# Second modulation moved from TensorE to ScalarE and GpSimd, and other units outside the ring

## What is computed

```python
mod = (silu(c) @ w_ada + b_ada).reshape(b, 6, 1, d)
shift1, scale1, gate1, shift2, scale2, gate2 = ...
h = rms_norm(x, norm1_g) * (1 + scale1) + shift1
proj = h @ w_in                      # conv, stick-breaking and forgetting heads
...                                  # attention of 6 + 6 heads, short convolution
x = x + gate1 * (y @ w_out)
h2 = rms_norm(x, norm2_g) * (1 + scale2) + shift2
x = x + gate2 * moe_ffn(h2, ...)     # per expert: w_mlp1 1024x2048 (8 MB), w_mlp2 1024x1024 (4 MB)
```

## Time and profile before

| | us |
|---|---|
| median of 3 runs | 1621.92 |
| the profiled execution | 1622.58 |
| its span | 1620.8 |
| TensorE busy | 1522.6 (94%) |
| VectorE busy | 669.7 (41%) |
| ScalarE busy | 456.2 (28%) |
| GpSimd busy | 113.7 (7%) |

### The profile page before, as it was taken

How to read it: one execution, slowest core, us unless ns; L and a number is a source line. 1 busy time by engine, 2 the same in 40 slices (tenths; PEclk the granted TensorE clock), 3 DMA queues, 4 the chain that set the end, 5 groups by cost and what they waited for, 6 DMA issues and landing times.

```text
span 1620.8 us, 21577 instructions
## 1 busy us (share of the span) xinstructions
PE 1522.6 (94%) x8585; PEld 868.8 (54%) x8585; DVE 669.7 (41%) x969; ACT 456.2 (28%) x760; POOL 113.7 (7%) x125
## 2 busy tenths in 40 slices
PE   7999999999999998999998989887999999999998
PEld 4888533333333333333332323223858998899986
DVE  4676632323322232232222222224866665465654
ACT  3565311011101110111110110003765444454443
POOL 4132200000000000000000000000520002200000
PEclk9999999999999999999999999998999999999999
DMA  9977999999999999999999999999537555465520
GB/s 352 381 217 274 385 385 426 426 409 415 426 426 426 426 425 427 427 425 425 427 426 426 425 426 426 426 424 346 187 104 223 188 190 191 143 210 183 182 104 27
DMA packets 113394, 534.27 MB, mean 330 GB/s; under 512 B 7013, under 2 KB 70140, under 8 KB 87376
## 3 DMA queue, kind: packets, MB, share of 16 engines
q1 hardware_dynamic: 111232, 529.97, 82.6%
q0 software_dynamic: 2000, 1.98, 0.4%
HBM read 530.87 MB, written 1.05 MB: 328 GB/s over the span
## 4 chain that ended last, share of the span: by engine, by line
PE 43%; DMA 17%; DVE 4%; ACT 2%; issue 1%; DVEq 0%
DMA ring<-in_w_mlp 17%; PE ps L1021 8%; PE ps L576 8%; PE ps L578 8%; PE ps L577 8%; PE ps L1039 5%; PE ps L1046 1%; PE ps L1478 1%; PE ps L1469 1%; DVE ps L2364 1%; DVE wm L1638 1%; PE ps L992 1%; DVE arena L2139 0%; DVE arena L2132 0%; DVE arena L2135 0%
## 5 line engine op out<-in xcount | busy, mean ns | idle before, releaser
L1021 PE MATMUL ps<-ring,arena 128*64 128x512 f32 x2024 | 483.8, 603 | 20.2 <-DMA ring<-in_w_mlp 18.5
L1021 PEld LDWEIGHTS ps<-ring,arena 128*64 128x64 f32 x2024 | 129.1, 136 | 255.7 <-issue 210.4
L1039 PE MATMUL ps<-ring,arena 128*64 128x512 f32 x1024 | 231.0, 597 | 16.6 <-DMA ring<-in_w_mlp 10.3
L1638 DVE TENSOR_TENSOR wl<-ring,wh 128x1024 fp32r<-128x1024 f32 x132 | 161.9, 1232 | 136.1 <-ACT wh L2527 136.1
L576 PE MATMUL ps<-hth,wh 128*128 128x256 f32 x704 | 201.0, 285 | 0.9 <-DVE htl L2319 0.8
L577 PE MATMUL ps<-htl,wh 128*128 128x256 f32 x704 | 198.7, 282 | 0.0
L578 PE MATMUL ps<-hth,wl 128*128 128x256 f32 x704 | 198.1, 281 | 0.0
L2119 DVE TENSOR_TENSOR arena<-ps,arena 128x1024 f32<-128x1024 f32 x68 | 83.2, 1224 | 251.6 <-PE ps L1046 246.1
L2527 ACT ACTIVATE wh<-ring 128x1024 fp32r<-128x1024 f32 x132 | 139.3, 1060 | 148.9 <-PE ps L578 148.8
L1039 PEld LDWEIGHTS ps<-ring,arena 128*64 128x64 f32 x1024 | 75.2, 137 | 164.7 <-issue 140.4
L2144 DVE TENSOR_TENSOR arena<-ps,arena 128x512 f32<-128x512 f32 x34 | 23.5, 691 | 334.0 <-PE ps L1039 330.9
(11 more groups left out here) (457 smaller groups left out, 1851.4 us busy)
## 6 DMA issues: line engine op xcount, KB each, us to landing
ring<-in_w_mlp SPq DMA_DIRECT2D x187, 2048.0 KB, 27.5
ring<-in_ffn_w_gate SPq DMA_DIRECT2D x22, 1024.0 KB, 5.4
ring<-in_ffn_w_up SPq DMA_DIRECT2D x22, 1024.0 KB, 5.4
ring<-in_ffn_w_down SPq DMA_DIRECT2D x22, 1024.0 KB, 4.8
ring<-in_w_ada SPq DMA_DIRECT2D x16, 1024.0 KB, 9.5
ring<-in_w_ada SPq DMA_DIRECT2D x16, 512.0 KB, 11.2
ring<-in_w_mlp SPq DMA_DIRECT2D x8, 1024.0 KB, 33.1
ring<-in_w_in SPq DMA_DIRECT2D x10, 768.0 KB, 12.7
```

Source lines behind the costliest of these rows:

```text
L1021: t = pe.matmul(PS[64 * g:64 * g + 64, HB[hb][ns], :], x[:, k8, :], u[:, f:f + 512], start=False, stop=k8 == 7)
L1039: t = pe.matmul(PS[64 * g:64 * g + 64, 3, :], a4[:, kc, 64 * kg:64 * kg + 64], u[:, c, g * 512:(g + 1) * 512], start=k8 == 0, stop=k8 == 7)
L1638: dve.tensor_tensor(l, src, h.bitcast(F32), ALU.subtract).then_inc(*V.tick((st, "lo", n)))
```

## The change

Five things at once:

- The eight units of the second modulation no longer go through TensorE. ScalarE multiplies each with its 128 values of silu(c) (`ada_scaled`, 128x2048, in place in the ring; unit 0 into slot 15, `row_sums`), VectorE adds `b_ada` to partition 0 of the sum, and GpSimd adds units 1 to 7 to `row_sums` (`summed`). So the sum over the 128 partitions is still open.
- It is made where it is used: gate1 by a product with ones (`gate_row`), shift2 by eight products with a column of ones, in place of `mod_row` and the four transposes.
- Unit k's slot is free only when GpSimd has added it, and slot 15 when shift2 is turned. `front_order` places the eight units one at a time between later pieces.
- Expert 0's last two w1 units are loaded into the ring. Outside stand w2 (0,3), loaded after the router's parts, and w1 (1,3), after "HL upper"; w2 (0,2) and w1 (1,2) come alone. For expert 0 `AT` lies elsewhere, and VectorE waits for its second pass ahead of the output.
- One DMA brings the 2048 biases instead of four; `conv_w_2` is loaded after expert 0's w2.

```diff
 def front_order():
-    for n, mods in enumerate(((0,), (1,), (2, 3), (4, 5), (6, 7))):
-        order += [("ada", 1, k) for k in mods] + [("in", *units[n])]
-    return order + [("in", *u) for u in units[5:]]
+    for n, k in enumerate((None, 0, 1, 2, 3, None, 4, 5, 6, 7, None)):
+        order += ([] if k is None else [("ada", k)]) + [("in", *units[n])]
+    return order
...
         if n == experts:
-            slots, at = [14, 15, 12, 13, 0, 1, 2, 3, 4, 5, 6, 7, 8, 9, 10, 11], 0
+            slots, at = [12, 13, 0, 1, 2, 3, 4, 5, 6, 7, 14, 15, 8, 9, 10, 11], 0
+            prior[GATE_SLOT] = ("row sums",)
...
+            if kind == "ada":
+                return [("summed", name[1])]
+            if kind == "row sums":
+                return ["shift2 turned"]
...
# TensorE
-            ada_unit(1, 0, 7)
             project(10, 11)
-            ada_unit(1, 1, 7)
             project(12)
-            ada_unit(1, 2, 7)
-            ada_unit(1, 3, 7)
             head_turn(0, SQ)
             project(13)
-            ada_unit(1, 4, 7)
-            ada_unit(1, 5, 7)
             cumulate()
             project(14)
             sb_z(0)
             turn_cum()
-            ada_unit(1, 6, 7)
-            ada_unit(1, 7, 7)
             project(15)
...
+            def gate_row(half):
+                return pe.matmul(PS[:, 6 + half, :], ones, row_sums[:, half * 512:half * 512 + 512], start=True, stop=True)
...
-            for cc in range(4):
-                t = pe.transpose(PS[:, 0, cc * 128:(cc + 1) * 128], strided(modr[:, 1, :], cc), ident)
+            for k in range(8):
+                t = pe.matmul(PS[:, 0, k:k + 1], strided(row_sums[:, 1024:2048], k), ones[:, 0:1], start=True, stop=True)
...
# VectorE
             los(8, 9)
+            dve.wait_ge(*done(("ada scaled", 0)))
+            dve.wait_ge(s_load["ab1"], 16)
+            first = row_sums[0:1, :]
+            dve.tensor_tensor(first, first, ring[0:1, (GATE_SLOT - 1) * UNIT:GATE_SLOT * UNIT], ALU.add).then_inc(
+                *V.tick(("summed", 0)))
             land(0)
...
-            mod_done(1, 7)
...
+                if e == 0:
+                    dve.wait_ge(*done(("w2b", 0)))
                 ob(V.tick, 0, 3, ("w2", e, 3), ("obf", e), ("obh", e), ("ob", e))
...
# ScalarE
+            def ada_scaled(*ks):
+                for k in ks:
+                    u = unit(("ada", k))
+                    act.wait_ge(*landed(("ada", k)))
+                    act.activation(u if k else row_sums, u, ACT.Copy, scale=cTp[:, k, 0:1]).then_inc(
+                        *S.tick(("ada scaled", k)))
...
             h_high(4, 5, 6, 7)
+            ada_scaled(0)
             his(8, 9)
             land(0)
+            ada_scaled(1)
             head_square(0, 0)
...
             his(13)
+            ada_scaled(2)
             forget_abs()
...
-            his(15, 16, 17)
+            his(15)
+            ada_scaled(3)
+            his(16)
+            ada_scaled(4)
+            his(17)
...
             his(19, 20)
+            ada_scaled(5)
             sb_log(0)
...
             his(24)
+            ada_scaled(6)
             head_root(1)
             land(5)
-            his(25, 26, 27)
+            his(25)
+            ada_scaled(7)
+            his(26, 27)
...
# GpSimd
+            def summed(k):
+                pool.wait_ge(*done(("ada scaled", k)))
+                pool.wait_ge(*done(("summed", k - 1)))
+                pool.wait_ge(*G.now())
+                pool.tensor_tensor(row_sums, row_sums, unit(("ada", k)), ALU.add).then_inc(*G.tick(("summed", k)))
+
             pool.wait_ge(*done("KZ zeroed"))
+            for k in range(1, 5):
+                summed(k)
+            pool.wait_ge(*G.now())
             pool.wait_ge(*done("cumT"))
...
             for g in range(2):
                 strict(g, ("sl", g), ("sa", g))
+            summed(5)
...
             for g in range(2):
                 strict(g, ("se", g), ("sb", g))
+            for k in (6, 7):
+                summed(k)
...
# SyncE
+            def outside(name, after, src):
+                sp.wait_ge(*done(after))
+                sp.dma_start(unit(name), src).then_inc(s_load[OUTSIDE[name]], 16)
...
                 if e == 1:
                     w1(1, (2, 4))
-                    for c in range(2):
-                        sp.wait_ge(*done(("parts", "HL upper")[c]))
-                        sp.dma_start(unit(("w1", 0, 6 + c)), I["w_mlp1"][0, 0][768:1024, :].rearrange(
-                            "(p c) n -> p c n", c=2)[:, c, :]).then_inc(s_load[f"w1_{6 + c}"], 16)
+                    outside(("w1", 1, 3), "HL upper", w1_rows(1, 2)[:, 2048:4096])
...
+                if e == 0:
+                    fill(("w2", 0, 0), lambda u: u, w2_rows(0, 0))
+                    outside(("w2", 0, 3), "parts", w2_rows(0, 2)[:, 2048:4096])
+                    fill(("w2", 0, 2), lambda u: u, w2_rows(0, 2)[:, 0:2048])
+                    continue
```

More of the change, by code:

```diff
@@ L119 @@
 STAGES = ["ada", "front", "oproj", "route", "moe", "moe2", "again", "mix", "ffn0", "pool", "ffn1", "last"]
-LOADS = ["c", "const", "const2", "cumr", "x", "rows", "ab", "fb", "rb", "cw", "cwr", "vr", "gq", "rw", "ab2", "b1", "b2", "ps", "final", "out", "again", "w1_6", "w1_7"]
-LAST_ALONE = tuple((NEXP - 1, k) for k in range(4, 8))
+LOADS = ["c", "const", "const2", "cumr", "x", "rows", "ab", "fb", "rb", "cw", "cwr", "vr", "gq", "rw", "ab1", "ab2", "b1", "b2", "ps", "final", "out", "again", "w2_03", "w1_13"]
+OUTSIDE = {("w2", 0, 3): "w2_03", ("w1", 1, 3): "w1_13"}
+ALONE = [("w1", NEXP - 1, k) for k in range(4, 8)] + [("w2", 0, 2), ("w1", 1, 2)]
 def w2_order(e):
@@ L136, in wide @@
 def wide(name):
-    return name[0] == "w1" and name[1:] not in LAST_ALONE or name[0] == "w2" and name[1] < NEXP - 1
+    return name not in ALONE and (name[0] == "w1" or name[0] == "w2" and name[1] < NEXP - 1)
 def front_order():
@@ L164, in ring_order @@
     for e in range(NEXP):
-        order += [("w1", e, k) for k in w1_order(e) if (e, k) != (0, 6)]
+        order += [("w1", e, k) for k in w1_order(e)]
         if e + 1 < NEXP:
@@ L239, in held @@
             return (name[0], name[1], name[2] - c) if c else name, c
+        row_sums = ring[:, GATE_SLOT * UNIT:(GATE_SLOT + 1) * UNIT]
         def landed(name):
-            if name in (("w1", 0, 6), ("w1", 0, 7)):
-                return s_load[f"w1_{name[2]}"], 16
+            if name in OUTSIDE:
+                return s_load[OUTSIDE[name]], 16
             s, n, _ = units[held(name)[0]]
@@ L590, in _ @@
             P = sig["pe_ada"]
[L592 to L598, removed]
             def turn(src, m, bank, name):
@@ L908, in _ @@
                     pe.wait_ge(*done(("yL", k)))
-                mod_row(6 + hf, 2, hf).then_inc(*P.tick(("gate1", hf)))
+                pe.wait_ge(*done(("summed", 7)))
+                gate_row(hf).then_inc(*P.tick(("gate1", hf)))
             out_piece(3)
@@ L1640, in mod_done @@
             def mod_done(b, bank):
-                last = {"A": ("modA", 3), "B": ("modB", 3), 1: ("ada", 1, 7), 2: ("scale2", 3), 3: ("gate2", 3)}
-                at = {"A": 0, "B": 2, 1: 1, 2: 2, 3: 0}[b]
+                last = {"A": ("modA", 3), "B": ("modB", 3), 2: ("scale2", 3), 3: ("gate2", 3)}
+                at = {"A": 0, "B": 2, 2: 2, 3: 0}[b]
                 dve.wait_ge(*done(last[b]))
@@ L3114, in _ @@
             small("cw", cwr, I["conv_w"][0, :, :])
-            for q in range(4):
-                small("ab", modr[32 * q:32 * q + 1, 1, :], I["b_ada"][:, 2048 + 512 * q:2560 + 512 * q])
+            small("ab1", ring[0:1, (GATE_SLOT - 1) * UNIT:GATE_SLOT * UNIT], I["b_ada"][:, 2048:4096])
             small("rb", rbrow, I["router_b"])
-            small("cwr", cwrow, I["conv_w_2"][0])
             for j in range(3):
@@ L3209, in _ @@
                     *G.tick("HL upper"))
+            pool.wait_ge(*done(("w2", 0, 3)))
+            small("cwr", cwrow, I["conv_w_2"][0])
             src, high, low, _, _ = piece("ab", 0)
```

54 lines of the change are left out of this document (27 added, 27 removed).

## The result

The changed kernel takes 1641.8 us (median of 4 runs, 1640.8 to 1643.7) against 1622.4 for the kernel before (4 runs): ratio 1.0127, 95% interval 1.0114 to 1.0139, 19.5 us slower. The forecast was 1629.4, +7.5, in a range up to 1635.0. The profiled execution took 1641.8 (span 1640.0). The direction was right, the size 2.6 times too small.

What follows compares the result with a forecast made beforehand. TensorE's progress was taken to bound the kernel up to about 372 us, the weight stream after. Front delays of +6.7 to +8.3, taken as +7.5, with the ring at 0, gave a median of 1629.4 us, range 1619.5 to 1635.0.

Steps and rivals of the forecast that it cites:

- no. 0: ScalarE's multiplication of modulation unit 0, ahead of pieces 8 and 9: said to move them back by 1.9 us.
- The bound: TensorE's progress sets the time up to about 372 us, the weights still to come after; front delays move the end one for one.
- It is the most that the change can give: Eight modulation units leave TensorE: 7.7 us at most, -2.5 retimed with ScalarE and GpSimd free of charge.
- (a): Pieces 8 to 11: multiplication 0 delays them, GpSimd's first sum then blocks VectorE; piece 10 ready at 57.8, +2.7 us.
- (b): Q and K transposes within a microsecond; multiplication 2 and GpSimd's second sum make the cumulative sums about 4.9 us later.
- (c): Second scores +3.0; sums 3 and 4 on pieces 16 and 17 and multiplication 5 make VectorE's first combination 6.7 us later.
- (d): Sums 6 and 7 fall over the last pieces, 118 to 128 us; TensorE's value products cover all but 1.6 us.
- Nothing either way, under 0.5 us: shift2's four transposes becoming eight one-column products, and the gate row's product with ones, change TensorE's time by under 0.5 us.
- (3): Rival, worse: waits line up, the last pieces' delay is uncovered and one more full block comes; +12.8, 1634.7 us, chance 0.15.
- (1): Rival: GpSimd's additions miss VectorE's pieces, only ScalarE's 1.9 and the row's 2.3 us are left; +2.2, 1624.1, chance 0.19.
- (2): Rival, faster: ScalarE's and GpSimd's work falls into idle time and TensorE keeps its saving; -2.5, 1619.4 us, chance 0.14.
- (4): Rival, nothing: the front's loss is hidden behind SyncE's queue at 134 us; a few in a hundred, counted within (1).

Runs made afterwards that it cites:

- e9: Changed kernel with GpSimd's additions and ScalarE's multiplications 1 to 7 on 64 of 2048 columns (sum incomplete, single run); 1624.1 us.
- e1: Changed kernel with GpSimd's seven additions on 64 of 2048 columns (sum incomplete); 1625.2 us.
- e4: Kernel before with only the new ring placement of expert units, its modulation units still on TensorE; 1622.7 us, ratio 0.9997.
- e16: Changed kernel with additions, multiplications 1 to 7 and VectorE's row on 64 columns, plus unused products in TensorE's waits (single run); 1625.7 us.
- e10: Changed kernel with additions on 64 columns and ScalarE's multiplications 2 and 5 moved behind the logs (single run); 1626.0 us.
- e11: Changed kernel with ten groups of unused products in TensorE's waits ahead of piece 10, the Q and K transposes and the cumulative sums; 1639.6 us.
- e8: Changed kernel with GpSimd's sums 6 and 7 moved later, over VectorE's forget masks and maxima; 1637.7 us.
- e5: Changed kernel with shift2's eight products on 64 columns each instead of 1; 1639.7 us.
- e13: Kernel before with eight unused 1-column products in front of its four transposes of shift2; 1624.6 us, ratio 1.0014.
- e12: Changed kernel with additions split into four of 512 columns, sums 6 and 7 moved later, shift2's products on 64 columns; 1631.4 us.
- e14: Kernel before with GpSimd's strict masks in pieces of 256 columns; 1620.5 us, ratio 0.9988.
- e15: Same three edits as e12, plus multiplications 2 and 5 moved behind the logs and unused products in TensorE's waits; 1631.6 us.

## Why the prediction was wrong

The 19.2 us at the bias, from the runs, up to gate2's issue counted from no. 0 on: 1.4 is no. 0's start at 46.95, where ScalarE began piece 8 at 45.59 before; 2.1 is no. 0 itself, VectorE's row and the clock behind TensorE's new wait, less what the removed units give back (e9, 90.98, against before, 88.84); 1.7 multiplications 1 to 7 (e1 against e9); 10.3 the additions (after against e1); 3.7 the router. e9 is one run with a late start, so the split of the 2.1 and 1.7 is the least certain.

- **The bound** was read rightly. The 372.39 issue moved by 21.0 and the end by 19.2, and e4 shows the ring part at 0 with the hole moved as described.
- **"It is the most that the change can give" (7.7, retimed to -2.5):** no run shows more than 1.1 of it (e16, from piece 10 on). TensorE was busy there in the trace before, but ScalarE and VectorE set most of the path; the modulation units were mostly fill. The -2.5 itself is neither shown nor refuted, as every run keeps no. 0 whole.
- **(a) and (b):** the block is as written, but (a) is 1.7 us short: piece 10 at 59.5 (57.8 forecast), since no. 0 and with it sum 1 (53.98 for 52.4) came 1.6 later than retimed. The cumulative sums' +5.3 (4.9 forecast) is partly luck: the Q and K transposes were 2.4 late and not within 1, and number 2, which (b) counts, fell into ScalarE's wait. One reading behind the block is loose: the fourth of its four cases, with 512 columns, ends 0.5 us after the addition, not 0.8; the pieces do end 0.8 after.
- **(c)** forecast 6.7 at the combination and 8.3 came, in part from other terms than it named. Number 5 is nearly as forecast (1.6 for 1.9, e10 against e1). Without any block it is 6.1 (e1), so sums 1 to 4 together add only 2.3 there; the later no. 0 and the lower clock behind the cumulative sums (e11: 1.4) carry most of the rest.
- **(d) is the step that failed.** "Covers all but 1.6 us" looked at TensorE's pieces only, and for these it holds: TensorE waits 0.22 us for piece 28 and takes piece 29 right behind the value products. But VectorE works in order, and behind pieces 28 and 29, held through two additions in a row, stand the forget mask, the maxima, two more pieces and the copies of the value products, with ScalarE's exponentials waiting beside them (9.43 us). TensorE's next scores wait 4.21 us for these copies, and nothing covers that. After and e1 differ by 3.6 us at the copies before these pieces (121.67 and 118.08) and by 9.1 at the mask (133.95 and 124.89): 5.5 us. e8 takes 4.1 back by moving just these two sums. A further 1.0 comes behind, at the lower clock after the 4.21 us.
- **"Nothing either way, under 0.5 us"** for the 1-column products is the second step that failed: 3.7 us lost between gate2 and the bias, of which e5 gives back 3.5 (from gate2's issue: 80.09 after, 76.57 in e5, 76.39 before). The clock was in no term of the sum.
- **Rivals.** (3) came nearest, with "(d) is not covered", but its +12.8 is less than the +15.5 at gate2 and the +19.5 of the end. (1) is refuted by the rows, (2) by the result, (4) by the +15.5 at gate2 with the end behind it. (3)'s chance of 0.15 was too small because (d) was argued and not retimed.

What stays open: how the blocks of sums 1 to 5 divide among them, what the removal of the units is worth with no. 0 gone too, and how much of the time the lower clock costs in an average execution.

## What to carry to other kernels

Work taken off a busy engine is worth what the retimed path gains, and where the engine was busy with fill that is little: here 1.1 us at most was seen of 7.7. Follow a held instruction not only to the engine that reads its result, but through everything behind it in its own engine's queue. A GpSimd instruction on SBUF can cost VectorE's instructions with two SBUF operands its whole length, so it is to be cut short (512 columns or 256) or laid over VectorE's PSUM reads; split masks gained 1.5 us even in the kernel before. Count TensorE's clock as a term of the sum where a change opens waits ahead of it, or puts products like these 1-column ones in place of wide ones.

## What the runs showed of the hardware

TensorE's clock fell to its lower level after waits: 4.28 us ahead of 59.49, where products then came every 0.325 us instead of 0.174. The Trainium skill ("TensorE: Matmul & The Clock Gate", "HAM oscillation — how this bites in real kernels") has products after such waits at the lower clock; the trace agrees. Not expected was that it also fell with hardly a wait, behind eight 1-column products (128x128 stationary) that the trace counts as 1.94 us of busy TensorE: in the changed kernel (191.5 to 203.7 us), and when they were put into the kernel before (e13). It fell in the router in 11 of the 12 profiles whose kernel has these products (not in e9), and in none of the six others (before, e4, e5, e12, e14, e15). So it isn't certain in every execution. Eight other 1-column products (line 955, 128x32 stationary) stand in the router of the kernel before as well; there they took 0.67 us and the clock stayed up behind them.
